# A gated three-branch encoder block on one core: which output branch runs beside which attention step, and where the fourth step's values stand

## What is computed

```
y_attn = _window_attention(q_a, k_a, v_a, attn_sinks[layer])
y_pool = _multiscale_pool(u_p, w_pool[layer], pool_scale[layer])
...
y_mem = _memory_attention(q_x, mem_k, mem_v)
gates = jax.nn.sigmoid((h @ w_gate[layer] + b_gate[layer]).astype(jnp.float32))
merged = (gates[:, :, 0] * (y_attn @ w_branch_attn[layer])
          + gates[:, :, 1] * (y_pool @ w_branch_pool[layer])
          + gates[:, :, 2] * (y_mem @ w_branch_mem[layer]))
x = x + merged @ w_out[layer]
hm = _rmsnorm(x, norm_mlp_g[layer])
x = x + jnp.square(jax.nn.relu(hm @ w_up[layer])) @ w_down[layer]
```

## Time and profile before

| | |
|---|---|
| median of 3 runs | 2721.77 us (2720.16 to 2725.88) |
| the profiled execution | 2719.93 us, of which the span is 2717.7 us |
| PE busy | 2590.3 us, 95% of the span |
| DVE busy | 1952.0 us, 72% |
| ACT busy | 1186.8 us, 44% |
| POOL busy | 580.0 us, 21% |

### The profile page before, as it was taken

The page is one execution under the profiler, slowest core; times in us unless marked ns, Lnnn a source line. Parts: engine busy times, 40 slices in busy tenths (PEclk is TensorE's granted clock), DMA queues, the critical chain, the costliest instruction groups (busy, mean ns, idle before and its releaser), DMA issues.

```text
span 2717.7 us, 33092 instructions
## 1 busy us (share of the span) xinstructions
PE 2590.3 (95%) x11961; PEld 2138.6 (79%) x11961; DVE 1952.0 (72%) x2809; ACT 1186.8 (44%) x2132; POOL 580.0 (21%) x517
## 2 busy tenths in 40 slices
PE   5999999999978999998898999999999999999998
PEld 4888888888866877876687888878888888888886
DVE  7777668786646778775678766686667767686897
ACT  5334534234434445543445544564456233242433
POOL 4344202441011234124354100000000212111100
PEclk8999999999988999999999999999999999999999
DMA  3777556764542565564778433543336666676752
GB/s 124 218 243 251 202 182 220 226 213 140 153 142 90 142 196 189 133 186 155 228 221 298 148 116 110 174 147 113 112 113 202 124 174 157 170 166 148 193 182 109
DMA packets 345549, 462.56 MB, mean 170 GB/s; under 512 B 32120, under 2 KB 228268, under 8 KB 345388
## 3 DMA queue, kind: packets, MB, share of 16 engines
q1 hardware_dynamic: 317740, 384.94, 45.0%
q0 software_dynamic: 27648, 75.51, 11.4%
HBM read 292.62 MB, written 167.77 MB: 169 GB/s over the span
## 4 chain that ended last, share of the span: by engine, by line
PE 77%; DVE 8%; DMA 6%; POOL 3%; issue 3%; ACT 1%; SPq 1%; DVEq 0%; POOLq 0%; ACTq 0%
PE ps L1841 25%; PE ps L1843 24%; PE ps L1842 24%; DMA t_d<-tin 2%; DMA rows_tm<-in_x 2%; PE ps L1846 1%; DVE s_lo L1241 1%; DMA tin<-in_w_down 1%; DVE res_lo L1245 1%; PE ps L2017 1%; PE ps L2042 1%; PE ps L1950 1%; DMA tin<-in_w_out 1%; POOL tin L1740 0%; POOL tin L1742 0%
## 5 line engine op out<-in xcount | busy, mean ns | idle before, releaser
L1841 PE MATMUL ps<-res_hi,s_hi 128*128 128x512 f32 x3080 | 1206.0, 392 | 29.3 <-issue 12.9
L1842 PE MATMUL ps<-res_lo,s_hi 128*128 128x512 f32 x3080 | 1202.1, 390 | 0.0
L1843 PE MATMUL ps<-res_hi,s_lo 128*128 128x512 f32 x3080 | 1202.1, 390 | 0.0
L1841 PEld LDWEIGHTS ps<-res_hi,s_hi 128*128 128x128 f32 x3080 | 580.9, 189 | 153.6 <-issue 19.1
L1843 PEld LDWEIGHTS ps<-res_hi,s_lo 128*128 128x128 f32 x3080 | 580.5, 188 | 121.1
L1842 PEld LDWEIGHTS ps<-res_lo,s_hi 128*128 128x128 f32 x3080 | 580.9, 189 | 119.5
L891 ACT ACTIVATE s_hi<-piece_f 128x512 fp32r<-128x512 f32 x440 | 275.8, 628 | 445.5 <-PE ps L1843 435.7
L891 ACT ACTIVATE s_hi<-s_sum 128x512 fp32r<-128x512 f32 x330 | 206.0, 627 | 349.1 <-PE ps L1843 320.7
L1241 DVE TENSOR_TENSOR s_lo<-piece_f,s_hi 128x512 fp32r<-128x512 f32 x440 | 332.7, 757 | 26.5 <-ACT s_hi L891 24.2
L1241 DVE TENSOR_TENSOR s_lo<-s_sum,s_hi 128x512 fp32r<-128x512 f32 x330 | 248.1, 753 | 101.7 <-ACT s_hi L891 101.6
L1715 POOL DMA_DIRECT2D rows_d<-c x96 | 83.2, 870 | 959.7 <-DVE c L1291 850.3
(11 more groups left out here) (163 smaller groups left out, 2712.9 us busy)
## 6 DMA issues: line engine op xcount, KB each, us to landing
proj_d<-c SPq DMA_DIRECT2D x152, 256.0 KB, 3.4
piece_f<-in_w_up SPq DMA_DIRECT2D x32, 1024.0 KB, 6.9
up_d<-c SPq DMA_DIRECT2D x128, 256.0 KB, 2.4
piece_f<-up_d SPq DMA_DIRECT2D x32, 1024.0 KB, 7.5
piece_f<-in_w_gate SPq DMA_DIRECT2D x24, 1024.0 KB, 6.3
temp<-proj_d SPq DMA_DIRECT2D x48, 512.0 KB, 5.2
rows_d<-c POOLq DMA_DIRECT2D x96, 256.0 KB, 4.5
t_d<-tin POOLq DMA_DIRECT2D x40, 512.0 KB, 4.2
```

What stands on the lines that cost most here:

```text
L1841: mm(dst, wh, xh, start=first, stop=False)
L1842: mm(dst, wh, xl, start=False, stop=False)
L1843: return mm(dst, wl, xh, start=False, stop=last)
```

## The change

From block 1 on, the memory branch of the block before moves from an attention block's first two steps to its last two, and the pool branch of the block itself to the first two. Block 0 has the same pieces as before. In the fourth step of every block PE's order becomes p0, p1, probabilities, q0, values, q1, where it was p0, p1, q0, probabilities, q1, values; and DVE makes the attention's low part ahead of the last gated tile.

```
-    r = 2 if i < 2 else 1
+    r = 1 if b == 0 or i < 2 else 2
     return [(r, b - 1 if r == 2 else b, 2 * (i % 2) + z) for z in range(2)]
...
-                gated(pieces[1], 1)
-                y0_low(b, i)
+                if i == TT - 1:
+                    y0_low(b, i)
+                    gated(pieces[1], 1)
+                else:
+                    gated(pieces[1], 1)
+                    y0_low(b, i)
...
-                            branch(q, 0)
-                            probs_across(b, i)
+                            if i < TT - 1:
+                                branch(q, 0)
+                                probs_across(b, i)
+                                branch(q, 1)
+                            else:
+                                probs_across(b, i)
+                                branch(q, 0)
+                        att_values(b, i)
+                        if i == TT - 1:
                             branch(q, 1)
-                        att_values(b, i)
```

## The result

The changed kernel takes 2730.99 us (median of 22 runs, 2720.51 to 2737.32), the kernel before 2722.56 us (median of 22 runs on the same chips, 2714.85 to 2728.62). The ratio is 1.0029 with a 95% interval of 1.0020 to 1.0038, so the change costs 5.4 to 10.3 us. The forecast was 2731.3 us, slower, with a range of 2721 to 2739 us. The profiled execution took 2733.98 us (span 2731.8 us), against 2719.93 us (2717.7 us) before.

A forecast was written before the change was run, and what follows sets the result against it. PE was taken to bound the kernel, with 77% of the chain that ended last. The terms -11.5 + 6.1 + 6.4 - 0.4 + 3.0 + 1.5 + 4.4 = +9.5 us, added to 2721.8, gave 2731.3 us, range 2721 to 2739.

The forecast's parts named there:

- A: Third steps of blocks 1 and 2: window sums leave them, so they take 14.24 us; gain 11.5 us.
- B: Starts of blocks 1 to 3: first branch tile waits for the fourth `y1_low`, 2.04 us later each; loss 6.1 us.
- C: Fourth steps, all four blocks: probabilities cross one tile earlier, so PE waits for scaled scores; loss 1.6 us each, 6.4 us.
- D: Fourth steps: values ahead of the last tile hide their way over ACT and DVE; gain 0.1 us each, 0.4 us.
- E: First two memory steps: window sums there hold DVE's two-SBUF-input operations; loss 1.5 us in each of two blocks, 3.0 us.
- F: Two block ends: second pool weight piece lands late behind `u_pad`, delaying ACT and PE; loss 1.5 us, bounds 0 and 3 each.
- G: Starts of blocks 1 to 3: longer waits lower PE's clock at two of three, 2.2 us each; loss 4.4 us.
- the faster rival: Fourth steps: DVE's halves scaled within 5.5 us of the scores' end, not 7.4, so early probabilities cost nothing; chance 0.06.
- the clock holds: Starts of blocks 1 to 3: PE's clock does not fall, leaving +5.1 us, 2726.9 us; chance 0.24.

The follow-up runs named there:

- the sums held back: Kernel before plus one wait: POOL's window sums start only when the attention branch's last low part of the block is done; 2710.36 us, ratio 0.9966.
- run with `u_pad` later: Changed kernel with the load of `u_pad` behind the third pool piece instead of the first; 2729.28 us, ratio 1.0026 against the kernel before.
- the sums in the second memory step: Kernel before with the window sums waiting for the scaled scores of the block's first memory step; 2712.14 us, ratio 0.9965.
- one memory piece first: Kernel before with, from block 1 on, one memory piece, four pool pieces, then the other three memory pieces; 2713.41 us, ratio 0.9967.
- the fourth step alone: Kernel before with only the fourth step's new order on PE and DVE, pieces in their old order; 2732.63 us, ratio 1.0035.
- PE kept busy: Changed kernel plus 11 unread 128x512 matmuls ahead of the first branch tile of blocks 1 to 3; 2727.15 us, ratio 1.0019 against the kernel before.
- the pieces alone: Kernel before with only the new order of the pieces, the fourth step in its old order; 2722.61 us, ratio 1.0007.

## Why the prediction was right, by its own steps

The forecast was +9.5 us, and the whole measured +7.9 us (0.29% of 2722.56 us), interval 5.4 to 10.3 us. In the stages of the profile, in us:

| step | forecast | measured | from |
|---|---|---|---|
| A, third steps | -11.5 | -11.5 | stages, and the run with the sums held back |
| B, the fourth `y1_low` | +6.1 | +5.8 | wait of 2.79 - 0.87 = 1.92, three times |
| C, early probabilities | +6.4 | +6.1 | 1.53, four times, alone |
| D, values ahead | -0.4 | +0.2 | 0.05, four times |
| E, sums in the memory steps | +3.0 | +1.7 | 9.65 - 8.79 = 0.86, twice |
| F, late weight piece | +1.5 | +0.9 | run with `u_pad` later |
| G, clock | +4.4 | +4.8 | 1.6, three times |

The measured column adds up to +8.0 us, and the mixers grew by 8.2 us; the rest is the start of block 0 (-0.5 us) and the end of the mixers (+0.7 us), which also vary from run to run: the wait for the last pieces at the end of the mixers took 7.1 us before, 7.9 us after and 7.5 to 10.4 us in the eight other traces. The errors of the single terms make 3.5 us regardless of sign, of which the sum keeps 1.5 us, as they partly cancel. That the time came out within 0.3 us of 2731.3 is luck: the forecast began at a median of 2721.8 us, and the kernel before measured 2722.6 us this time.

*A, B and C* hold as argued. DVE's second scaling in the fourth step of block 1:

```profile
993.54 0.69 DVE L1434 TENSOR_TENSOR scores<-scores,rd 128x512 f32<-128x512 f32 x1
```

It ended at 993.54 + 0.69 = 994.23 us, 8.6 us after the start of its scores at 985.61 us; in the kernel before it was also 991.37 - 982.75 = 8.6 us. DVE's chain did not move, so the faster rival has fallen at the point that was named for it. The wait for it came in two pieces, 0.82 and 0.36 us, 1.18 us in all and not the 1.6 us that the prediction wanted to see. Most of the rest of the 1.53 us is that the transposes now run as two groups of 0.66 us, where one of 1.03 us stood.

*D* was given a small gain and has none. The covered way of the values was not on PE's path: what comes off the memory step is put on the fourth step.

*E* was right in place, wrong in the operation, and too large. All of the four two-tensor operations were named as candidates and none got longer. The low part of the weight took 1.21 us beside the sums. The scaling took 2.06 us, because it only changed one partner for another: before it was held by an addition of gated tiles, and 1.23 us is what it takes alone. The 0.86 us came from `nb`, 1.21 us instead of 0.17 us, which had been counted nowhere. That the forecast named the first memory step and a loss of the right sign was so in part luck. The assumption that the reads of PSUM between them aren't held is right: the maximum took 1.23 us, the gated tile 0.67 to 0.69 us. Only the first memory step pays; in the second DVE's slack took what there was, as the prediction allowed.

*F* is two thirds of its estimate: the piece was late, and by less. The time of its load came from a row of block 0 (6.3 us). The three loads of `u_pad` for the later blocks, 1056 KB, have a median of 9.3 us in the kernel before, and the two in question took 5.3 us in the changed kernel, so that row was a lucky choice.

*G* was put at two falls of 2.2 us and is three of 1.6 us. Both errors are opposite and nearly cancel, which is luck. The rival "the clock holds" did not come true at any of the three starts of this execution, and it did at one of three, behind a wait as long, in the run with `u_pad` later. The rows that the prediction weighed could not decide it: the waits of 2.94 and 2.41 us stand in block 0 of every trace, and other traces show the opposite behind each (last section). So three falls in three starts is what this trace shows, not what every execution must.

One slip does not touch the sum: the prediction gave `y1_low` and `att_scale` new line numbers, but in the changed kernel they keep L1453 and L1434.

The window sums ran from 1004.85 to 1020.02 us. The fourth step's scores came 985.61 - 982.75 = 2.86 us later than before, so in the frame of before this is 1002.0 to 1017.2 us, as forecast (1002 to 1018).

Three kernels beat both: the sums held back (0.9966), the sums in the second memory step (0.9965), and one memory piece first (0.9967). They can't be told from each other; each saves about 9 to 10 us against the kernel before, by a few lines or one. The one gain of the change was that the sums left the third step, and none of its other effects was needed for that.

## What to carry to other kernels

Before moving a stage's work to free a shared resource, ask whether the disturber can be moved instead: one wait on POOL gave the whole gain that the reordering paid back at three other places. When the tile that stands first behind a chain of small operations changes its input, count from the last of them and add the clock to the wait: here 1.9 us of added wait became 3.5 us where the clock fell (block 3). A duration read beside another engine's work is not the operation's own; look for the same operation in a stage where that engine is idle before costing an overlap.

## What the hardware showed unexpectedly

An operation of DVE of 128x4 with one SBUF input, TENSOR_SCALAR, was held by a window sum on POOL: 1.21 us in the first memory steps of blocks 1 and 2 after the change, 0.17 us in every memory step before, and 1.01 us with one memory piece first. The Trainium skill, "SBUF — State Buffer", section "Who interferes with whom", names `tensor_scalar` among the operations that can take the shared pair of ports when their operands allow it, beside those with two SBUF inputs; this trace agrees as to which operations are held. The prediction cited the same section for the later one to issue being the one blocked, and found its rows to agree. They agree in the length only. By the start times DVE came first: the maximum 0.29 us ahead of the window sum, `nb` 0.10 us ahead (1004.75 and 1004.85). Both ended 0.02 to 0.03 us behind the window sum's end. With one memory piece first `nb` started 0.11 us behind, and ended the same way.

A wait of the same length did not always lower the clock. The clearest case lies outside the change: the same wait of 2.94 us for `w_lo` stands in block 0 of all ten traces. The clock fell there in five (the kernels before and after, the fourth step alone, the sums in the second memory step, PE kept busy) and held in the other five, as here, in the run with `u_pad` later:

```profile
843.30 0.39 PE L1845 MATMUL ps<-w_hi,m_hi 128*128 128x256 f32 x1 [2.94 <-DVE w_lo L1410]
```

```profile
844.00:847.00 3.00, 3.00 (x27) 2.71 (x27) 0.00 (x0) 0.77 (x2) 0.00 (x0) 1.00 0.00 0
```

The wait of 2.41 us ahead of it was followed by a fall in three traces of ten (after, the fourth step alone, PE kept busy). At the block starts, behind 2.79 us it fell at block 3 of the changed kernel, and in the run with `u_pad` later it fell behind 2.80 and 2.79 us and held behind 2.79 us; with the pieces alone it fell behind 2.77 us. Behind every wait of 3.08 us or more at a block's start it fell (3.08, 3.20, 3.32, 3.50 us). What decides below 3 us is open; it is not the length of the wait alone. The price had more sizes than one: 1.6 us at six starts (first matmul of the tile 0.47 us), 2.7 and 2.9 us at two (0.77 us). The first matmul is no sure sign of it: in the third steps of the kernel before it took 0.80 and 0.79 us, and the excess over the waits was 6.16 - 3.23 = 2.9 us and 5.37 - 3.22 = 2.2 us.

The window sums on POOL take 1.05 to 1.08 us where nothing holds them and 2.01 to 2.17 us beside an operation of DVE with two SBUF inputs (the low part of the weight, the scaling), so POOL pays in the same coin: the ten took 13.2 us in the third step and 15.2 us in the memory steps.
